# Per-head sums in the RWKV stage: one product with a 128x128 block-diagonal of ones, or two 64x64 products

## What is computed

```python
kk = kk / jnp.maximum(jnp.sqrt(jnp.sum(kk * kk, axis=-1, keepdims=True)), 1e-12)
...
y = rwkv7_recurrence(rh, dh, kh, vh, -kk, kk * ah)
mu = jnp.mean(y, axis=-1, keepdims=True)
var = jnp.mean(jnp.square(y - mu), axis=-1, keepdims=True)
y = ((y - mu) * lax.rsqrt(var + LNX_EPS)).reshape(B, S, D)
...
bonus = jnp.sum(rh * kh * r_k.astype(f32), axis=-1, keepdims=True) * vh
```

## Time and profile before

| | |
|---|---|
| median of 3 runs | 3438.9 us (3435.59 to 3452.97) |
| profiled execution | 3442.61 us, of which the span of the trace is 3440.9 us |
| PE busy | 3300.1 us, 96% of the span |
| DVE, ACT, POOL busy | 2276.5, 1561.4, 348.2 us |
| mean granted TensorE clock | 0.975 of full |
| RWKV loop, `i` = 0 to 7 | from about 1024 to 1439 us of the span |
| products with `bones` | 64, of which 60 in that loop or behind it |

### The profile page before, as it was taken

How to read it: one execution, slowest core, us unless ns; L and a number is a source line. 1 busy time by engine, 2 the same in 40 slices (tenths; PEclk the granted TensorE clock), 3 DMA queues, 4 the chain that set the end, 5 groups by cost and what they waited for, 6 DMA issues and landing times.

```text
span 3440.9 us, 58456 instructions
## 1 busy us (share of the span) xinstructions
PE 3300.1 (96%) x19942; PEld 2865.9 (83%) x19942; DVE 2276.5 (66%) x3244; ACT 1561.4 (45%) x2195; POOL 348.2 (10%) x524
## 2 busy tenths in 40 slices
PE   7999999989989999999999999999999999999998
PEld 6887777878878888888888888888778888888887
DVE  6657666588764666577575767776566766667576
ACT  5543444467535556444343434444344433434343
POOL 2001022000123233120000000100011100000002
PEclk9999999989999999999999999999999999999999
DMA  6654455456750001166666666667534666666664
GB/s 186 171 141 121 122 154 165 123 152 182 211 169 13 29 21 30 43 184 183 187 182 190 185 190 188 186 177 189 140 114 135 183 189 181 187 184 186 184 183 147
DMA packets 1001253, 523.81 MB, mean 152 GB/s; under 512 B 25750, under 2 KB 996396, under 8 KB 1000620
## 3 DMA queue, kind: packets, MB, share of 16 engines
q1 hardware_dynamic: 995756, 507.99, 52.5%
q0 software_dynamic: 4560, 13.05, 1.1%
q10 hardware_dynamic: 816, 1.11, 0.1%
HBM read 513.69 MB, written 8.39 MB: 152 GB/s over the span
## 4 chain that ended last, share of the span: by engine, by line
PE 84%; DVE 7%; ACT 5%; issue 3%; DMA 0%; POOL 0%; ACTq 0%; DVEq 0%; SPq 0%; POOLq 0%; PEldq 0%
PE proj L301 47%; PE proj L303 24%; PE side L2340 2%; PE side L2369 1%; PE side L2230 1%; DVE w_low L257 1%; ACT w_high L270 1%; DVE g L311 1%; PE side L807 1%; DVE w_low L273 1%; PE side L2214 0%; PE side L2388 0%; PE side L2216 0%; ACT w_high L251 0%; ACT g L2110 0%
## 5 line engine op out<-in xcount | busy, mean ns | idle before, releaser
L301 PE MATMUL proj<-b_pair,w_high 128*128 128x512 f32 x3872 | 1388.1, 402 | 22.0 <-DVE b_pair L1077 9.6
L301 PE MATMUL proj<-a_pair,w_high 128*128 128x512 f32 x3664 | 1296.7, 398 | 40.0 <-DVE a_pair L1682 19.7
L273 DVE TENSOR_TENSOR w_low<-w_raw,w_high 128x1024 fp32r<-128x1024 f32 x688 | 839.5, 1227 | 434.9 <-ACT w_high L270 431.2
L303 PE MATMUL proj<-b_pair,w_low 128*128 128x256 f32 x3872 | 1094.1, 283 | 0.0
L303 PE MATMUL proj<-a_pair,w_low 128*128 128x256 f32 x3664 | 1031.2, 281 | 0.0
L270 ACT ACTIVATE w_high<-w_raw 128x1024 fp32r<-128x1024 f32 x696 | 733.3, 1058 | 567.1 <-PE proj L303 561.8
L301 PEld LDWEIGHTS proj<-b_pair,w_high 128*128 128x128 f32 x3872 | 736.7, 190 | 205.6 <-issue 16.0
L301 PEld LDWEIGHTS proj<-a_pair,w_high 128*128 128x128 f32 x3664 | 691.9, 189 | 206.5 <-issue 21.7
L303 PEld LDWEIGHTS proj<-b_pair,w_low 128*128 128x128 f32 x3872 | 741.5, 191 | 0.2
L303 PEld LDWEIGHTS proj<-a_pair,w_low 128*128 128x128 f32 x3664 | 697.4, 190 | 0.1
L257 DVE TENSOR_TENSOR w_low<-w_raw,w_high 128x1024 fp32r<-128x1024 f32 x276 | 348.0, 1268 | 251.2 <-ACT w_high L251 245.5
(11 more groups left out here) (574 smaller groups left out, 2991.7 us busy)
## 6 DMA issues: line engine op xcount, KB each, us to landing
w_raw<-in_mlp_w_up_dram SPq DMA_DIRECT2D x256, 512.0 KB, 4.3
w_raw<-in_mlp_w_down_dram SPq DMA_DIRECT2D x256, 512.0 KB, 4.0
w_raw<-in_w_in_dram SPq DMA_DIRECT2D x112, 512.0 KB, 3.9
w_raw<-in_rwkv_w_rkv_dram SPq DMA_DIRECT2D x96, 512.0 KB, 4.1
w_raw<-in_w_kvf_dram SPq DMA_DIRECT2D x64, 512.0 KB, 4.1
w_raw<-in_w_out_dram SPq DMA_DIRECT2D x32, 512.0 KB, 3.9
w_raw<-in_rwkv_w_o_dram SPq DMA_DIRECT2D x32, 512.0 KB, 4.2
w_raw<-in_fox_w_q_dram SPq DMA_DIRECT2D x32, 512.0 KB, 4.0
```

What stands on the lines that cost most here:

```text
L273: eng.tensor_tensor(wl[slot][:], raw[slot][:], wh[slot][:].bitcast(F32), ALU.subtract)\
L301: pe.matmul(ps[bank][:, :].rearrange("p (a n) -> p a n", a=2), wh[slot][:, k, :], pair[:, :, kk, :], start=kk == 0, stop=False)
L303: mm = pe.matmul(ps[bank][:, 0:S], wl[slot][:, k, :], pair[:, 0, kk, :], start=False, stop=kk == KT - 1)
```

## The change

Each of the four helpers calls a new function, `head_sums`, which issues two products of 64 rows and 64 columns: one for partitions 0 to 63, one for 64 to 127. Their weights are the two diagonal blocks of `bones`, all ones. Both write the same PSUM region as before, each its own half of the partitions; the semaphore is raised by the second. Semaphores, waits, order and all other engines stay as they are.

```diff
+        def head_sums(pe, out_, src):
+            for h in range(2):
+                mm = pe.matmul(out_[rng(h)], bones[rng(h), rng(h)], src[rng(h)], start=True, stop=True)
+            return mm
+
...
-                    pe.matmul(early(j, s)[0], bones[:], RW_T[s]["sq"], start=True, stop=True).then_inc(sem("rw_ss"), 1)
+                    head_sums(pe, early(j, s)[0], RW_T[s]["sq"]).then_inc(sem("rw_ss"), 1)
...
-                    pe.matmul(early(j, s)[1], bones[:], RW_T[s]["t"], start=True, stop=True).then_inc(sem("rw_bs"), 1)
+                    head_sums(pe, early(j, s)[1], RW_T[s]["t"]).then_inc(sem("rw_bs"), 1)
...
-                    pe.matmul(ps[s][:, 0:S], bones[:], RW_C[s]["y"], start=True, stop=True).then_inc(sem("rw_mu"), 1)
+                    head_sums(pe, ps[s][:, 0:S], RW_C[s]["y"]).then_inc(sem("rw_mu"), 1)
...
-                    pe.matmul(ps[s][:, 0:S], bones[:], RW_C[s]["ysq"], start=True, stop=True).then_inc(sem("rw_var"), 1)
+                    head_sums(pe, ps[s][:, 0:S], RW_C[s]["ysq"]).then_inc(sem("rw_var"), 1)
```

## The result

| | before | after |
|---|---|---|
| median of 20 runs | 3440.88 us (3431.65 to 3452.97) | 3452.11 us (3434.37 to 3462.58) |
| ratio after to before, with its 95% interval | | 1.0029 (1.0017 to 1.004) |
| profiled execution, span | 3440.9 us | 3445.5 us |

The change makes the kernel slower by 0.3%, some 10 us (6 to 14). The forecast was 6.5 us, within 0.5%, and a time between 3437 and 3460; the median of 3452.1 lies in that range.

What follows compares the result with a forecast made beforehand. The prediction took PE, busy 96% of the span, to bound the kernel. Changes of array part at means, squares, spreads and outside the loop summed to 6.5 us of loss on the median 3438.9, giving 3445.4 us, range 3437 to 3460.

Steps and rivals of the forecast that it cites:

- The halves side by side: In each split product the two 64*64 halves overlap on the array, so it still takes 0.43 us.
- rival 1: Halves of each split product run in series, 0.43 us more per product: 3469 us, chance 0.10.
- The 0.43 spacing: The two products of means still start 0.43 to 0.48 us apart after the change.
- The price of a change of part: PE switching array part: 0.14 us into a 64*64 part, 0.20 into the whole array, 0.34 together.
- `bonus` beside the chain: At level 5, bonus saves PE 0.20 us each time, but beside DVE work, so nothing was counted.
- The sum: Loss of 6.5 us: means 2.4, squares 2.4, spreads 1.1, last iteration's spreads 0.3, products outside the loop 0.3.
- the second, the clock: Short PE stops bring falls to 1.2 GHz in five iterations, 1.3 us each: 6.5 us more, 3452 us, chance 0.09.
- Rivals 3 and 4: Waits at levels 3 to 5 absorb half PE's delay: 3441 us, 0.06; 64*64 at twice pace: over 0.5% gain, 0.01.

Runs made afterwards that it cites:

- filled pair: Kernel before and changed kernel, both with unread products in PE's pause ahead of line 2343: 0.9975 and 0.9995 of before; the profiled stretch differs by 5.4 us.
- profiled pair: First traces of the kernel before and the changed kernel, pause unfilled; from level 4 of iteration 0 to that of 7 they differ by 9.7 us.
- second pair: Second traces of the same two unfilled kernels, before and changed; over the same stretch they differ by 6.2 us.
- fill_joined: Kernel before with only bonus split, line 2309's products moved ahead of lines 2303 and 2304, and PE's pause filled: 3431.4 us, 0.9982 of before.

## Why the prediction was right

- **The halves side by side** held: 0.65 us for four matmuls, and rival 1 (3469 us) is out. The 0.43 spacing with the first load bare was 0.48, as forecast. Two row halves that write different partitions of one PSUM bank run together here, against the rule of the Trainium skill (TensorEngine Tiling (Array Packing), "Gotcha 1: PSUM Pressure") that the prediction had weighed; line 2343 had shown it already.
- **The price of a change of part** held: 0.14 and 0.20, in all three helpers with whole-array neighbours. Each measured 0.35, 0.35, 0.19 for 0.34, 0.34, 0.18.
- **`bonus` beside the chain** held: no gain in the iteration, with 0.21 us less of PE and a longer wait behind it.
- **The sum** was 6.5, of which 5.8 (seven `means`, six `squares`, seven `spreads`) lies in the stretch of the filled pair, and that shows 5.4. The other 0.7 (`squares` of pair 1, and the products outside the loop) no run isolates.
- **What may be missing** lies between the 6.5 and the measured 10. The measured interval, 6 to 14, includes the forecast, so there may be nothing. Of the rivals only the second, the clock, could fill it. It gave 4.3 us in the profiled pair and 0.8 in the second pair, where the rival had priced 6.5 and got a chance of 0.09. Its price of 1.3 us for a fall was that of the short ones; one of 17 us cost 7.0. That chance looks too small now: I had argued that each iteration has changes of part anyway and keeps its clock, and had not looked where in the iteration the clock falls. It falls behind the wait for ACT, which every iteration has and which has nothing to do with changes of part. Whether the change brings more falls on average, or the profiled pair did so by chance, stays open. With it stays open whether 6.5 was right or some 3 us short.
- **Rivals 3 and 4** fell: nothing was absorbed at levels 3 to 5, and nothing ran at twice the pace.

## What to carry to other kernels

A small product that takes another part of the array than its neighbours cost a stop of 0.09 us and a bare weight load of 0.05 to 0.10 at each end here, 0.34 in all, and it gains nothing if the whole-array product already did both halves in one pass. Before changing or merging such places, look for a wait in front of them: a change of part that lies in a wait costs no stop, so there is less to gain from taking it away, and a new order can bring another wait, as that for ACT at line 2319. When one engine's short wait comes once per iteration, look at the granted clock right behind it; filling PE's pause with idle products took 0.25% off here, about as much as the change had cost.

## What the runs showed of the hardware

- A 64x64 product of 16 columns between two whole-array products takes 0.21 us from its start to that of the next, the stop of 0.09 included, where 16 columns at the pace of the earlier trace rows are 0.03 for both of its matmuls.
- Around a pause of PE of 1.3 us, which each iteration of 52 us has, the clock fell to 1.2 GHz in 2 to 5 of six iterations in the traces of before and after; some falls lasted 17 us. With the pause filled by six matmuls, none of three traces (before filled, after filled and `fill_joined`) had a fall from level 4 of iteration 0 to level 4 of iteration 7.
- The kernel before, unchanged, had medians from 3434.5 to 3442.9 us in three comparisons, and 0.9984 of itself within one.
